# Two transformer blocks on one core: the first out product finished token block by token block, and the MLP's first pair multiplied in two halves

## The reference, cut to what matters

```
y = jnp.concatenate([y_a, y_b], axis=-1)
return y @ w_out                                  # end of mixer()
...
    x = x + rmsnorm(y, norm_mix_post[l])
    h = rmsnorm(x, norm_ffn_pre[l])
    y = conv_mlp(h, w_up[l], conv_ffn[l], w_down[l])

def conv_mlp(h, w_up, conv_w, w_down):
    u = dwconv3(h @ w_up, conv_w)                 # 1024 -> 5632, then a width-3 convolution over tokens
    gate, val = jnp.split(u, 2, axis=-1)
    return (jax.nn.silu(gate) * val) @ w_down     # 2816 -> 1024
```

## Time and profile before

| | us |
|---|---|
| time before, median of 3 | 689.34 |
| the three runs | 689.18, 689.34, 690.75 |
| span of the profiled execution | 686.0 |
| TensorE busy in the span | 636.9 (93%) |
| VectorE, ScalarE busy | 379.4 (55%), 277.6 (40%) |

### The profile page before, as it was taken

How to read it: one execution, slowest core, us unless ns; L and a number is a source line. 1 busy time by engine, 2 the same in 40 slices (tenths; PEclk the granted TensorE clock), 3 DMA queues, 4 the chain that set the end, 5 groups by cost and what they waited for, 6 DMA issues and landing times.

```text
span 686.0 us, 11096 instructions
## 1 busy us (share of the span) xinstructions
PE 636.9 (93%) x4347; PEld 481.4 (70%) x4347; DVE 379.4 (55%) x666; ACT 277.6 (40%) x431; POOL 56.3 (8%) x81
## 2 busy tenths in 40 slices
PE   7999999999999999999999999999999866768895
PEld 4999997799999999996697788744444332324364
DVE  6686965668766677767768465542222220203195
ACT  6764373556555555545755721311111000000193
POOL 1000000400000000003084610000000000000010
PEclk9999999999999999999999999999999998989998
DMA  8944541757755555204903548999899999999931
GB/s 324 349 144 148 199 147 33 262 159 244 234 187 187 188 187 188 97 0 140 330 38 122 188 182 308 364 425 427 362 431 426 428 427 428 427 425 428 408 140 61
DMA packets 55209, 174.75 MB, mean 255 GB/s; under 512 B 4743, under 2 KB 29443, under 8 KB 48899
## 3 DMA queue, kind: packets, MB, share of 16 engines
q1 hardware_dynamic: 54496, 172.54, 65.9%
q10 hardware_dynamic: 674, 1.69, 0.7%
HBM read 173.17 MB, written 1.05 MB: 254 GB/s over the span
## 4 chain that ended last, share of the span: by engine, by line
PE 68%; DMA 19%; DVE 7%; ACT 3%; issue 2%; another core or an unknown queue 0%; POOLq 0%; POOL 0%; DVEq 0%; ACTq 0%
PE ps L1801 15%; PE ps L1803 15%; PE ps L1802 15%; DMA arena<-in_w_moe_dram 14%; PE ps L2318 5%; DMA W<-in_w_moe_dram 4%; PE ps L2302 2%; PE ps L2378 2%; PE ps L1998 2%; PE ps L2324 1%; PE ps L2425 1%; PE ps L2146 1%; DVE arena L1458 1%; PE ps L2097 1%; PE ps L2161 1%
## 5 line engine op out<-in xcount | busy, mean ns | idle before, releaser
L1801 PE MATMUL ps<-hT_high,w_up_parts 128*128 128x256 f32 x352 | 99.8, 283 | 0.0
L1803 PE MATMUL ps<-hT_high,w_up_parts 128*128 128x256 f32 x352 | 99.6, 283 | 0.0
L1802 PE MATMUL ps<-hT_low,w_up_parts 128*128 128x256 f32 x352 | 99.6, 283 | 0.0
L1801 PEld LDWEIGHTS ps<-hT_high,w_up_parts 128*128 128x128 f32 x352 | 67.5, 192 | 0.5
L1802 PEld LDWEIGHTS ps<-hT_low,w_up_parts 128*128 128x128 f32 x352 | 67.5, 192 | 0.4
L1803 PEld LDWEIGHTS ps<-hT_high,w_up_parts 128*128 128x128 f32 x352 | 67.5, 192 | 0.0
L1289 DVE TENSOR_TENSOR w_up_parts<-W,w_up_parts 128x1024 fp32r<-128x1024 f32 x44 | 52.8, 1227 | 25.5 <-ACT w_up_parts L818 25.5
L818 ACT CAST w_up_parts<-W 128x1024 fp32r<-128x1024 f32 x44 | 44.7, 1047 | 29.7 <-PE ps L1803 29.7
L988 ACT ACTIVATE sg<-ps 128x256 f32<-128x256 f32 x9 | 3.5, 384 | 122.3 <-PE ps L2318 122.3
L1801 PE MATMUL ps<-h_high,dense_high 128*128 128x256 f32 x160 | 45.7, 286 | 0.0
L2318 PE MATMUL ps<-W,junk 128*32 128x512 f32 x304 | 37.2, 618 | 9.0 <-DMA W<-in_w_moe_dram 9.0
(11 more groups left out here) (480 smaller groups left out, 1355.4 us busy)
## 6 DMA issues: line engine op xcount, KB each, us to landing
W<-in_w_moe_dram SPq DMA_DIRECT2D x24, 2048.0 KB, 22.8
arena<-in_w_moe_dram SPq DMA_DIRECT2D x17, 2048.0 KB, 29.9
W<-in_w_up_dram SPq DMA_DIRECT2D x22, 1024.0 KB, 8.8
W<-in_w_in_dram SPq DMA_DIRECT2D x8, 2048.0 KB, 10.8
W<-in_w_down_dram SPq DMA_DIRECT2D x11, 1024.0 KB, 5.0
hh<-in_w_moe_dram SPq DMA_DIRECT2D x4, 2048.0 KB, 30.2
W<-in_w_out_dram SPq DMA_DIRECT2D x2, 2048.0 KB, 9.0
W<-in_w_o_dram SPq DMA_DIRECT2D x2, 2048.0 KB, 8.3
```

Source lines behind the costliest of these rows:

```text
L1801: pe.matmul(o, lhs[0], rhs[0], start=first, stop=False, skip_group_check=True)
L1802: pe.matmul(o, lhs[0], rhs[1], start=False, stop=False, skip_group_check=True)
L1803: return pe.matmul(o, lhs[1], rhs[0], start=False, stop=last_k, skip_group_check=True)
```

## The change

1. **Out product.** Its 96 matmuls stand in another order: block 0 is finished after 60 of them and not after 72. `turn_h(1, 0)` stands ahead of the last 12.
2. **First pair.** `up(0, 0)` is replaced by `up_first(0)`, the products of the pair for the 128 tokens of block 0, and `up_first(1)`, the same for block 1: 96 matmuls with 128 moving columns each, both with all the stationary operands of the pair. `turn_h(1, 1)` stands between them. Only `up_first(1)` raises `up_used`.
3. **Fillers.** Both `keep_busy` and the 24 matmuls of L1940 are gone. The zeroing of the accumulators has 8 matmuls and not 4.
4. **ACT and DVE.** The quarters of block 0 are turned out and rounded right behind block 0's part of the hand-over, ahead of block 1's. All four chunks of pair 0's weights are split ahead of the hand-over, where two were split behind it.
5. The tile y1_high lies elsewhere in the arena, since the weights of chunks 2 and 3 are now written while it is read.

```diff
-        y1 = [v3(rounded("y1_high", arena_at, Q_IN, 2 * D), KD), v3(rounded("y1_low", hh_at, 2 * D, 2 * D), KD)]
+        y1 = [v3(rounded("y1_high", arena_at, NAR - UNIT, 2 * D), KD), v3(rounded("y1_low", hh_at, 2 * D, 2 * D), KD)]
...
# ACT
-            split_up(0, 0, 0, (0, 1))
+            split_up(0, 0, 0)
             for b in range(TB):
                 hand_over(0, b)
-            act.dma_start(gbc[:], a["norm_ffn_post"][0:1, :].broadcast_to([P, D])).then_inc(sig("gbc_landed"), 16)
-            for j in range(1, 4):
-                round_h(j)
+                if b == 1:
+                    act.dma_start(gbc[:], a["norm_ffn_post"][0:1, :].broadcast_to([P, D])).then_inc(sig("gbc_landed"), 16)
+                round_h(2 * b)
+                round_h(2 * b + 1)
...
# PE
-            for half in range(2):
-                for b in range(TB):
-                    for k in range(4):
...
-            turn_h(1, 0)
-            keep_busy(3, 8)
-            for k in range(24):
-                pe.matmul(ps[:, 3, 0:P], y1[0][:, k % KD, 0:P], y1[0][:, k % KD, 0:P], start=True, stop=True, skip_group_check=True)
+            out_rows(0, 0, range(4))
+            out_rows(1, 0, range(4))
+            out_rows(0, 1, range(4))
+            pe.wait_ge(sig("y1_low"), 2)
+            out_rows(0, 0, range(4, KD))
+            out_rows(0, 1, range(4, KD)).then_inc(sig("y_done"), 1)
+            out_rows(1, 1, range(4))
+            pe.wait_ge(sig("y1_low"), 3)
+            out_rows(1, 0, range(4, KD))
+            turn_h(1, 0)
+            out_rows(1, 1, range(4, KD)).then_inc(sig("y_done"), 1)
+
+            def up_first(b):
+
+                for c in range(4):
+                    pe.wait_ge(sig("up_low"), c + 1)
+                    i, g = divmod(c, 2)
+                    o = ps[:, i, 256 * g + b * P:256 * g + (b + 1) * P]
+                    for k in range(KD):
+                        if c == 0 and k % 4 == 0:
+                            pe.wait_ge(sig("hT_low"), 2 * b + k // 4 + 1)
+                        last = product(o, [t[:, c, k, :] for t in w_up_hl], [t[:, k, b * P:(b + 1) * P] for t in hT_hl],
+                                       k == 0, k == KD - 1)
+                    if b == 1:
+                        last.then_inc(sig("up_used"), 1)
+
+            up_first(0)
             turn_h(1, 1)
-            pe.wait_ge(sig("hT_ready"), 4 + 2)
-            keep_busy(0, 8)
-
             pe.wait_ge(sig("x_ready"), 2)
-            for n in range(4):
-                pe.matmul(ps[:, 4 + n, :], zb[:, 0:P], zb[:], start=True, stop=False, skip_group_check=True)
+            for n in range(8):
+                pe.matmul(ps[:, 4 + n % 4, :], zb[:, 0:P], zb[:], start=(n < 4), stop=False, skip_group_check=True)
+            up_first(1)
...
-            up(0, 0)
             with pe.Fori(0, NPAIR // 2) as i:
```

More of the change, by code:

```diff
@@ L719, in hand_over @@
                    .then_inc(sig("ystd_ready"), 1)
-                if b == 1 and r == 0:
-                    round_h(0)
                 c = 4 * (r + 1) + b
@@ L849, in conv_mlp @@
                 act.copy(uact_hl[0][:, q], uact[q]).then_inc(sig("uact_high"), 1)
-            act.wait_ge(sig("x_ready"), 2)
-            split_up(0, 0, 0, (2, 3))
             conv_mlp(0, 0, 0)
@@ L1128, in hand_over @@
                                              ALU.add).then_inc(sig("yms_ready"), 1)
-                    if b == 1:
+                    if b == 1 and r == 1:
                         turn_out(r + 1, gain, 0)
@@ L1144, in hand_over @@
                                              ALU.add).then_inc(sig("xms_ready"), 1)
-                    if b == 1 and r == 0:
-                        lower_h(0)
                     dve.wait_ge(sig("std_ready"), 2 * (r + 1) + b + 1)
@@ L1151, in hand_over @@
                                       ALU.mult).then_inc(sig("hn_ready"), 1)
-                turn_out(r + 1, gain, 2)
-                turn_out(r + 1, gain, 3)
+                    if r == 0:
+                        for j in (2 * b, 2 * b + 1):
+                            turn_out(r + 1, gain, j)
+                        for j in (2 * b, 2 * b + 1):
+                            lower_h(j)
+                if r == 1:
+                    turn_out(r + 1, gain, 2)
+                    turn_out(r + 1, gain, 3)
             def lower_h(j):
@@ L1290, in split_up @@
                                       w_up_hl[0][:, c].bitcast(F32), ALU.subtract).then_inc(sig("up_low"), 1)
-            split_up(0, 0, (0, 1))
+            split_up(0, 0)
             hand_over(0, "norm_ffn_pre")
-            for j in range(1, 4):
-                lower_h(j)
             def conv_mlp(p, q, h, more=True):
@@ L1330, in _ @@
             dve.sem_inc(sig("uact_ready"), 1)
-            split_up(0, 0, (2, 3))
             conv_mlp(0, 0, 0)
@@ L1937, in _, with out_rows @@
-            turn_h(1, 0)
-            keep_busy(3, 8)
-            for k in range(24):
-                pe.matmul(ps[:, 3, 0:P], y1[0][:, k % KD, 0:P], y1[0][:, k % KD, 0:P], start=True, stop=True, skip_group_check=True)
+            def out_rows(b, half, ks):
+                for k in ks:
+                    pe.wait_ge(sig("dense_low"), 4 * (6 + half) + k // 2 + 1)
+                    last = product(ps[:, 4 + 2 * b + half, :], [t[:, k, b * P:(b + 1) * P] for t in y1],
+                                   [t[:, k, :] for t in panel_hl(6 + half)], k == 0, k == KD - 1)
+                return last
@@ L1941, in _ @@
+            up_first(0)
             turn_h(1, 1)
-            pe.wait_ge(sig("hT_ready"), 4 + 2)
-            keep_busy(0, 8)
             pe.wait_ge(sig("x_ready"), 2)
-            for n in range(4):
-                pe.matmul(ps[:, 4 + n, :], zb[:, 0:P], zb[:], start=True, stop=False, skip_group_check=True)
+            for n in range(8):
+                pe.matmul(ps[:, 4 + n % 4, :], zb[:, 0:P], zb[:], start=(n < 4), stop=False, skip_group_check=True)
+            up_first(1)
             def up(p, q):
-                if not (isinstance(p, int) and p == 0):
-                    pe.wait_ge(sig("tap_done"), p * 8 - 7)
+                pe.wait_ge(sig("tap_done"), p * 8 - 7)
@@ L1956, in up @@
                     for k in range(KD):
-                        if isinstance(p, int) and p == 0 and c == 0 and k % 4 == 0:
-                            pe.wait_ge(sig("hT_low"), 3 + k // 4)
                         last = product(o, [t[:, c, k, :] for t in w_up_hl], [t[:, k, :] for t in hT_hl], k == 0, k == KD - 1)
```

## The result

| | us |
|---|---|
| before, median of 8 runs | 690.12 (689.18 to 690.75) |
| after, median of 8 runs | 692.01 (690.89 to 693.53) |
| ratio after / before | 1.0028, 95% interval 1.0018 to 1.0039 |
| in us | +1.9, 1.3 to 2.7 |
| profiled execution of after | time 690.89, span 688.9 |

The kernel is slower, by a little less than the 0.3% that the prediction had set as the line, with an interval clear of zero. The time lies 0.4 us from the forecast, but that closeness is partly luck: the forecast was 689.34 + 3.1, the measurement is 690.12 + 1.9.

What follows compares the result with a forecast made beforehand. TensorE waiting some 10 us for norms between out product and MLP was the bound. Filling it with 11.2 us of thin work moved the last matmul from 141.40 to 144.5; 689.34 + 3.1 gave 692.4 us, range 690.2 to 696.5.

Steps and rivals of the forecast that it cites:

- smaller shift: Rival, 16%: thin step 0.111 and a slightly shorter step from second transposes to next product; shift 1.8 us, 691.1, counted as no change.
- Step 5: First thin pass, up_first(0): 96 matmuls at 0.117 us take 11.2 us, 119.15 to 130.4.
- step 8: Second thin pass, up_first(1): 94 x 0.117 = 11.0 us, last matmul starts at 144.5 against 141.40 before, shift 3.1 us.
- The other edits: Moved splits, removed fillers, queue waits and y1_high's new place: all hidden or without cost beyond the counted steps.
- Same shape and engines: Reason given for y1_high's new place in the arena costing nothing.
- 3.3 us between span and median: Gap between profiled span 686.0 and the runs' median, carried over from span 689.1 to the forecast time.
- The first fillers: The 8 zero and 24 thin matmuls removed from the wait: 3.4 us at full clock, nothing won by removing them.
- 10 us of waiting: TensorE's wait for norms between out product and MLP, some 10 us, the most the change could win.
- A thin matmul at 0.064: Rival, 9%: 128 columns take their columns' time, the weight load hidden; last matmul at 134.4, 7.0 us earlier, 682.3.
- A fall of the clock in the thin matmuls: Rival, 11%: clock drops during 22.5 us of thin matmuls, 2 us a drop, up to 22; about 697.
- 81 ns at 128 columns: The skill page's sustained matmul step, against the 0.117 us taken; by it the sum would be 685.5.

Runs made afterwards that it cites:

- thin_only: The kernel before with only its first pair made in two passes of 128 columns behind the transposes: 698.86 us, ratio 1.0132.
- order_wide: The changed kernel with its first pair as one wide pass of 256 columns again and 26 zero matmuls filling the wait: 687.88 us, ratio 0.9970 to before.
- half_thin: The changed kernel with only chunks 0 and 1 split into thin passes, chunks 2 and 3 wide behind them: 686.75 us, ratio 0.9956 to before.
- y1_place: The kernel before with only y1_high's new address: 686.62 us beside 688.29 of the kernel before, one profiled run.
- half_thin_again: A second profile of half_thin, nothing changed: 686.66 us beside 689.17 of the kernel before.
- after_again: The changed kernel profiled once more, nothing changed: 690.59 us.

## Why the prediction was right, and where it was not

**The mechanism holds, step by step.** VectorE starts block 0 at 109.72 (predicted 110.0), the first transposes stand at 115.17 (115.4), the first pass begins at 118.87 (119.15), the second transposes at 129.54 (130.4) with TensorE as the one that is late, the next product at 132.41 (133.2), the last thin one at 143.04 (144.5). That the split doubles the stationary loads is shown by thin_only (+9.1), and that this, beyond the cover, is the whole loss is shown by order_wide and half_thin, which keep everything else and are faster than before.

**Step 5 and step 8: the thin matmul was mis-sized.** It was taken at 0.117 from the fillers of L1940 and costs 0.1115, close to the 0.111 of the earlier trace rows. Over 192 matmuls that is 1.1 us, by the positions of the two passes 1.2, which is most of the 1.5 us between 144.5 and 143.04. In this the rival "smaller shift" had the right size.

**The other edits: y1_high's place was costed at nothing.** In after the 84th matmul of the out product starts 18.94 behind the first, in the profiles of before 19.32 to 19.35. That is 0.4 us, and the first pass starts 0.3 earlier than forecast. "Same shape and engines" was the failed reason: the place of an operand was not in it. y1_place shows that it is the place; why is open.

**The baseline: a fall of the clock was taken as part of the kernel.** Against the profile of before the last thin matmul is 1.6 us later, and the MLP's end 1.4, not 3.1. The profile of before held a fall of 1.6 to 1.7 us at 125 that three of four further profiles of it lack there. Against those, the change adds 223.9 (the mean of the three of after) - 220.85 = 3.1 us. Then the profile of after has its own fall near 367, so the spans differ by 2.9 us again. The predicted 3.1 is thus what the ruler shows without falls, by terms that were not all right. At the last thin matmul the sum closes: the baseline was 1.7 too late (141.40 - 95.72 = 45.7 behind T0, without the fall 44.0), which hid as much loss, the step took back 1.2 and the place 0.3, and 3.1 + 1.7 - 1.5 = 3.3 is what the last thin matmul is late (47.3 - 44.0). That two misses of about the same size cancelled is luck.

**The sum.** Timed, the shift is 1.9 (1.3 to 2.7), below 3.1, and the mean spans of the profiles agree with it: 686.6 for the five of the kernel before, 688.8 for the three of after, 2.2 apart. On the ruler the difference of the means is 223.9 - 221.5 = 2.4, since two of the five have the fall at 125. Ahead of T0 after is 0.4 shorter; two of the five, and none of the three, have the fall near 12. Behind the MLP it is 0.2 longer. So falls that differ in number between the profiles can make 1.9 out of 3.1. That is argued, not shown: the profiles are few, and the other timed runs have none. The prediction's 3.3 us between span and median was not what lies around the span, which is 690.89 - 688.9 = 2.0; the rest is that a profiled execution can be one of the faster ones (690.89 is the lowest of the eight).

**Two of its figures do not follow from its rows.** The first fillers take 4.5 us (119.17 to 120.71 + 2.98) and not 3.4; nothing hung on it. And the "10 us of waiting" were 11.6 us less 16 transposes and 4 zeros at full clock (1.9 + 0.9), so some 9, and 1.7 of these were the fall. The wait that the new order leaves is shorter still: half_thin's 48 thin matmuls, 5.35 us, fill all but 0.19 of it.

**The rivals.** A thin matmul at 0.064 is excluded by 0.1115 in after and 0.1117 in thin_only. A fall of the clock in the thin matmuls is excluded as well: 1.00 in 119.2 to 130.4 and 133.2 to 144.5, and in thin_only's 21 us. The forecast's estimate by the Trainium skill ("TensorE: Matmul & The Clock Gate", "Back-to-back issue gap", 81 ns at 128 columns) does not hold for these 4-byte operands. By the same page's "LDWEIGHTS" (columns / 1.2) a weight load of 128 columns is estimated at 107 ns, near the 111.5 ns measured for a step.

**What the idea is worth.** Under cover, a chunk made in two passes turns 24 x 0.120 behind the cover into 24 x 0.1115: 0.2 us. Beyond the cover it costs another 24 x 0.1115 = 2.7 us. Two chunks fit in the 5.6 us of block 1's norm, four do not. On the ruler half_thin gains 220.85 - 219.44 = 1.4 over the kernel before without a fall, of which order_wide has 1.0, and y1_high's place 0.4 of that. Timed they gain 3.0 and 2.1. The surplus of 1.6 and 1.1 is about the size of one fall, and their three profiles have neither the one at 125 nor the one near 367. The mean span of the kernel before, in which each profile has one of the two, is 2.4 us above order_wide's and 2.5 above half_thin's mean. That the new order keeps these falls away is not shown: after has it and the fall near 367 in two of three, and y1_place with the old order lacks both. Half_thin is the fastest version found; its lead over order_wide is 0.4 on the ruler, and their timed intervals overlap.

## What to carry to other kernels

Work that is split to fill a wait must be priced by the stationary operands that it loads twice: halving the moving columns from 256 to 128 saved 7% of a matmul here, so a wait of 5.6 us took half a pair's first pass and paid 0.2 us a chunk. Fill a wait up to its end and not beyond, because the part that sticks out is paid in full. And before a clock fall in one profile is built into a baseline, take a second profile of the same kernel.

## What the runs showed of the hardware

- The step of a stream of matmuls with 4-byte operands and a new stationary operand each time, at full granted clock: 0.111 us at 36 columns, 0.1115 at 128 (after, thin_only), 0.120 at 256, 0.227 or 0.232 at 512.
- Putting the tile of a stationary operand (y1_high) at another place in SBUF, with the same shape and layout, changed the step at 512 columns from 0.232 to 0.227 (y1_place), but for the first ten or so steps, which stayed at 0.231. The cause was not tested.
- The granted clock fell to half (1.2 GHz) for some 3.4 us at one of two places in each of five profiles of one kernel, 240 us apart, and at neither in y1_place, order_wide, half_thin, half_thin_again and after_again. Three of the 14 profiles have it near 12 too, and all have it for 13 to 24 us in all between 550 and 680. Ahead of 125 TensorE had been idle for 1.1 us, in executions with the fall and without it, and for 21 us of thin matmuls the clock stayed at 1.00 (thin_only). What decides the place, or whether it comes at all, stays open.
